# Norm sums inside the chunk loop, a reordered last unit and a two-tile start, in the dense layers of a two-block transformer kernel

## What is computed

```python
def rms_norm(x, gain):
    y = x * lax.rsqrt(jnp.mean(x * x, axis=-1, keepdims=True) + EPS)
    return y * gain

def conv_ffn(x, w_up, conv_w, conv_b, w_down):       # layers "ffn0" and "ffn1"
    hid = causal_dwconv(x @ w_up, conv_w, conv_b)
    gate, val = jnp.split(hid, 2, axis=-1)
    return (jax.nn.gelu(gate) * val) @ w_down

def swiglu(h, w_gate, w_up, w_down):                 # layer "ffn2"
    return (jax.nn.silu(h @ w_gate) * (h @ w_up)) @ w_down

# first block, twice:  mix -> x = x + rms_norm(mix, g[1]); h = rms_norm(x, g[2])
#                      x = x + rms_norm(conv_ffn(h), g[3])
# second block: mla attention + swiglu, then s5 mixer + mixture of 8 experts
```

## Time and profile before

| | us |
|---|---|
| median of 3 runs | 2239.53 |
| lowest, highest | 2238.09, 2240.12 |
| the profiled execution | 2240.73 |
| its span (first to last instruction) | 2238.6 |

### The profile page before, as it was taken

The page is one execution under the profiler, slowest core; times in us unless marked ns, Lnnn a source line. Parts: engine busy times, 40 slices in busy tenths (PEclk is TensorE's granted clock), DMA queues, the critical chain, the costliest instruction groups (busy, mean ns, idle before and its releaser), DMA issues.

```text
span 2238.6 us, 67369 instructions
## 1 busy us (share of the span) xinstructions
PE 2171.1 (97%) x30382; PEld 2005.3 (90%) x30382; DVE 847.0 (38%) x2103; ACT 467.1 (21%) x1074; POOL 24.5 (1%) x43
## 2 busy tenths in 40 slices
PE   9999999999999999999987999999999999999998
PEld 8888998757899876899976889999999999999998
DVE  4247665314867645567769220101010101010102
ACT  3432112113311135210033121111111111111112
POOL 1000000000000000000000000000000000000000
PEclk9899999999999999999998999999999999999999
DMA  9241444241244323343331259999999999999996
GB/s 391 90 169 64 163 170 159 74 181 58 113 164 154 136 79 132 151 156 153 150 127 59 93 182 405 392 396 392 397 389 399 393 395 391 397 383 396 388 417 262
DMA packets 78399, 535.02 MB, mean 239 GB/s; under 512 B 8913, under 2 KB 9042, under 8 KB 41938
## 3 DMA queue, kind: packets, MB, share of 16 engines
q1 hardware_dynamic: 74450, 519.82, 59.0%
q0 software_dynamic: 3840, 13.63, 1.7%
HBM read 523.20 MB, written 10.22 MB: 238 GB/s over the span
## 4 chain that ended last, share of the span: by engine, by line
PE 61%; DVE 3%; ACT 1%; issue 1%; DVEq 0%; ACTq 0%
PE ps L1792 26%; PE ps L1804 13%; PE ps L1179 6%; PE ps L1109 4%; PE ps L1212 4%; PE ps L1574 2%; PE ps L1557 1%; DVE scr L2467 0%; PE ps L1743 0%; PE ps L1756 0%; PE ps L1765 0%; PE ps L1444 0%; PE ps L1430 0%; PE ps L1511 0%; PE ps L1406 0%
## 5 line engine op out<-in xcount | busy, mean ns | idle before, releaser
L1792 PE MATMUL ps<-scr,slot 128*64 128x96 f32 x14336 | 638.1, 246 | 0.7 <-issue 0.7
L1792 PEld LDWEIGHTS ps<-scr,slot 128*64 128x64 f32 x14336 | 612.7, 137 | 2.4 <-issue 2.3
L2616 DVE TENSOR_TENSOR scr<-scr,ps 128x96 f32<-128x96 f32 x224 | 56.8, 254 | 764.9 <-ACT scr L960 764.9
L1804 PE MATMUL ps<-scr,slot 128*64 128x96 f32 x7168 | 341.9, 246 | 1.6 <-issue 1.6
L1804 PEld LDWEIGHTS ps<-scr,slot 128*64 128x64 f32 x7168 | 317.3, 137 | 1.8 <-issue 1.8
L1212 PE MATMUL ps<-scr,slot 128*128 128x256 f32 x1056 | 241.8, 383 | 7.9 <-DVE scr L2284 7.9
L1212 PEld LDWEIGHTS ps<-scr,slot 128*128 128x128 f32 x1056 | 198.0, 192 | 34.3 <-DVE scr L2284 9.5
L960 ACT ACTIVATE scr<-ps 128x96 f32<-128x96 f32 x224 | 56.1, 250 | 784.9 <-PE ps L1792 784.9
L1179 PE MATMUL ps<-vtok,slot 128*128 128x128 f32 x1056 | 140.1, 276 | 2.7 <-DVE vtok L2224 2.7
L1179 PEld LDWEIGHTS ps<-vtok,slot 128*128 128x128 f32 x1056 | 128.9, 192 | 3.5 <-DVE vtok L2224 3.5
L1179 PE MATMUL ps<-vtok,proj 128*128 128x128 f32 x1056 | 129.9, 277 | 0.0
(11 more groups left out here) (408 smaller groups left out, 2069.7 us busy)
## 6 DMA issues: line engine op xcount, KB each, us to landing
slot<-in_w_moe SPq DMA_DIRECT2D x224, 1024.0 KB, 7.0
slot<-in_w_moe SPq DMA_DIRECT2D x224, 512.0 KB, 7.0
slot<-in_w_ffn SPq DMA_DIRECT2D x33, 3072.0 KB, 10.4
slot<-in_w_even_in SPq DMA_DIRECT2D x3, 3072.0 KB, 27.2
slot<-in_w_odd_qk SPq DMA_DIRECT2D x2, 3072.0 KB, 10.8
slot<-in_w_s_glu SPq DMA_DIRECT2D x2, 3072.0 KB, 11.6
slot<-in_w_odd_v SPq DMA_DIRECT2D x2, 2048.0 KB, 8.0
slot<-in_w_even_in SPq DMA_DIRECT2D x2, 1536.0 KB, 10.7
```

The lines of the kernel that those rows point to most:

```text
L1792: m = pe.matmul(gate_up(j, k)[s:s + STRIP], ups[j][:, o:o + STRIP], xg[:, c], start=c == 0, stop=c == KD - 1, skip_group_check=True)
L1804: m = pe.matmul(y_sum(d)[s:s + STRIP], downs[j][:, o:o + STRIP], hid[j][:, 0:CAP], start=False, stop=False, skip_group_check=True)
L2616: dve.tensor_tensor(hid[f % 4][:, 0:CAP], gbuf[f % 4][:, 0:CAP], gate_up(f, 1), ALU.mult).then_inc(hid_ready, 1)
```

## The change

Three edits, in all places where they apply.

1. Input norm of the dense layers (n2, n6, m1). VectorE's adds of the squares go (`add_squares`, and in ffn2 the `add_square` calls), the three norms leave `PRESUMMED`, and TensorE sums all eight squares with the matrix of ones: the square of chunk c-1 behind the plain products of chunk c, that of chunk 7 at the end. `summed(0, 0)` then waits for each input sum by itself instead of for all four.
2. Last unit: up(10, 0), up(10, 1), down(9, 0), down(9, 1) instead of up, down, up, down.
3. `first_tiles`: the projections behind ffn0 and ffn1 fill tile 0 and tile 1 together, two products for each chunk of `hT`. In the fox projection tile 1 so comes before the eight gate products (L1455) and the norm's sum; before, it came after them.

```diff
-PRESUMMED = ("n1", "n2", "n3", "n4", "n5", "n6", "n7", "m0", "m1")
+PRESUMMED = ("n1", "n3", "n4", "n5", "n7", "m0")
...
+            def add_square(name, c):
+                if c == 0:
+                    pe.wait_ge(rms_ready, NORM_NO[name])
+                pe.wait_ge(sq_ready, SQ0[name] + c + 1)
+                m = pe.matmul(sum_of(name), ones[:, :], sq[:, c], start=c == 0, stop=c == KD - 1,
+                              skip_group_check=True)
+                if c == KD - 1:
+                    m.then_inc(sum_ready, 1)
...
+            def first_tiles(phase, name):
+                w, n = need(phase, 0), TILE0[phase]
+                pe.wait_ge(tile_taken, n + 2 - WORK)
+                for c in range(KD):
+                    pe.wait_ge(h_ready, H0[name] + c + 1)
+                    for i in range(2):
+                        o = (i * KD + c) * P
+                        m = pe.matmul(work(n + i), w[:, o:o + P], hT[:, c], start=c == 0,
+                                      stop=c == KD - 1, skip_group_check=True)
+                        if c == KD - 1:
+                            m.then_inc(tile_ready, 1)
...
+                    def inputs(n):
+                        if u == k == 0:
+                            pe.wait_ge(combined, X_SUM0[phase] + n)
                     pe.wait_ge(combined, W_SUM0[phase][2 * u + k] + 4)
+                    inputs(1)
                     four(k, P5, t1, s1, True)
+                    inputs(2)
                     four(k, P6, t2, s2, False)
...
                                   x_half[0][c // 4][:, c % 4], start=c == 0, stop=c % 4 == 3,
                                   skip_group_check=True)
-                presummed_total(LATE[phase])
-                pe.wait_ge(combined, X_SUM0[phase] + 4)
+                    if c:
+                        add_square(LATE[phase], c - 1)
+                add_square(LATE[phase], KD - 1)
                 summed(0, 0)
                 summed(0, 1)
                 for u in range(1, UNITS):
                     need(phase, u)
                     up(u, 0)
-                    down(u - 1, 0)
-                    up(u, 1)
+                    if u < UNITS - 1:
+                        down(u - 1, 0)
+                        up(u, 1)
+                    else:
+                        up(u, 1)
+                        down(u - 1, 0)
                     down(u - 1, 1)
...
             def fox():
-                linear("odd_qk", hT, h_ready, H0["n4"], range(1))
+                first_tiles("odd_qk", "n4")
...
                 presummed_total("n4")
-                linear("odd_qk", hT, h_ready, H0["n4"], range(1, 3))
+                linear("odd_qk", hT, h_ready, H0["n4"], range(2, 3))
...
             def mla():
-                linear("mla_in", hT, h_ready, H0["m0"], range(2))
+                first_tiles("mla_in", "m0")
...
-                    if c >= 3:
-                        add_square("m1", c - 2)
                 gain_tile("m1", KD - 1, "ffn_norm", 0)
-                add_square("m1", KD - 2)
...
             post_norm("n1", 8)
-            add_squares("n2")
             input_sums("ffn0")
...
             post_norm("n5", 40)
-            add_squares("n6")
             input_sums("ffn1")
```

More of the change, by code:

```diff
@@ L1191, in summed @@
                     s1, s2, s3, s4 = x_sum
+                    def inputs(n):
+                        if u == k == 0:
+                            pe.wait_ge(combined, X_SUM0[phase] + n)
                     pe.wait_ge(combined, W_SUM0[phase][2 * u + k] + 4)
+                    inputs(1)
                     four(k, P5, t1, s1, True)
+                    inputs(2)
                     four(k, P6, t2, s2, False)
+                    inputs(3)
                     four(k, P7, t3, s3, False)
+                    inputs(4)
                     four(k, P3, w_block(phase, u, k, 1, 1), s4, False)
```

## The result

The changed kernel takes 2226.4 us (median of four, 2223.3 to 2229.2) where the kernel before takes 2238.8 in the same session: a ratio of 0.9939 with an interval of 0.9924 to 0.9954. That is 13.7 us by the ratio and 12.4 by the medians, against 17.4 forecast. It is faster, and the time lies inside the stated range of 2217.5 to 2227.5, at its upper end. It lies outside the forecast's own range (2219.5 to 2224.5), and next to the 2226.7 of the rival by which the clock does not follow; that this rival's mechanism isn't what happened is shown further down.

A forecast was written before the change was run, and what follows sets the result against it. TensorE, busy for 97% of the span, bounds the kernel through its work, waits and low clock. -2.1 - 2.1 - 1.6 + 2.6 - 9.8 - 0.3 - 4.1 = -17.4 us from 2239.5 gives 2222.1, range 2217.5 to 2227.5.

The forecast's parts named there:

- the rival by which the clock does not follow: Stalls go, but the three low-clock stretches stay or turn up elsewhere; 4.7 us not gained, 2226.7 us; chance 0.17.
- Edit 1, squares between chunks: Start of ffn0 and ffn1: 0.875 us per chunk, input sums ready in time, new waits free; 2.1 us gained in each.
- The low clock in ffn1: Stretch behind ffn1's chunks, at a clock of 0.90: no gap, so no low clock expected after the change; 1.6 us gained.
- ffn2, +2.6: Start of ffn2: six more square products on the path, where VectorE's adds had been hidden; 2.6 us lost.
- Edit 2, -4.9 each and -0.3: Last unit: reordering removes a 3.3 us stall and 1.57 of low clock in ffn0 and ffn1; 0.3 gained in ffn2.
- The thin margin: Last unit of ffn0 and ffn1: two down products cover the chain to the hidden layer with only 0.1 us to spare.
- The rival by which the chain grows with the moved products: Last unit: the chain behind up(10, 1) grows, so only half of the 9.8 us is gained; 2227 us; chance 0.05.
- Edit 3, -2.15 and -2.05: Fox and mla projections: tiles 0 and 1 together take 6.9 us; 2.15 us gained in fox, 2.05 in mla.
- the mla margin: Mla projection: VectorE's adds end 0.3 us before the norm's sum is asked for; if used up, edit 3 gives 3.6.
- The clock term, 4.7 us: Low clock behind stalls goes: 1.6 us at ffn1's start plus 2 x 1.57 in the last units of ffn0 and ffn1.
- They shift as a block: Stages behind the layers (s5, router, experts) start from TensorE's events, weight loads too, so they move together; no loss there.
- The slower rival: Interleaved products run at 1.2 GHz, their 35 us of work taking 70; sum becomes +17, 2257 us; chance 0.02.

The follow-up runs named there:

- the version that undoes it: The changed kernel with ffn2's squares added on VectorE as before the change: 2222.8 us, ratio 0.9930 against the kernel before.
- the waits: The kernel before with 37 waits for something already there at the start of TensorE's program: 2242.0 us, ratio 1.0014.
- 104 instructions ahead: The changed kernel with ffn2's squares back on VectorE, plus 26 tiny unused products at the start of TensorE's program: 2223.5 us, ratio 0.9920.
- the single edits: Edits 1, 2 and 3 each made alone, against the kernel before: 2239.2, 2231.6 and 2236.3 us, ratios 0.9994, 0.9958 and 0.9990.

## Why the prediction was right where it was, and wrong where it wasn't

The terms inside the layers came true almost one by one. The number is too large by 4 to 5 us, because of the stages behind and, by an amount that stays open, the clock.

- **Edit 1, squares between chunks: right, with a gain forecast a little too large.** Chunks at the pace of 0.88 us, sums ready in time, waits at no cost. The piece took 7.33 us where 7.27 was worked out, and gained 1.9 in each layer where 2.1 was forecast. The rest is the cold weight load of 0.12 us, which I had counted with this piece and which lies behind its end (the -0.1 of unit 0 in the table).
- **The low clock in ffn1: 1.6 forecast, 1.7 in the first pair of profiles.** As a term of the time it holds only for some executions, see below.
- **ffn2, +2.6: right**, as 2.6 in three traces, and gone in the three of the version that undoes it. It was the one loss that was forecast, and it was real.
- **Edit 2, -4.9 each and -0.3: right** in all six traces that have it, against the first profile of before. Against the later profiles, whose stall brought no low clock, it is -3.4 each. The thin margin was as worked out. The rival by which the chain grows with the moved products falls: the hidden layer was there 0.2 us early.
- **Edit 3, -2.15 and -2.05: 2.0 each.** In fox the reciprocal came 1.5 us later from the projection's start, where 1.3 was worked out, and the margin of 1.2 was as forecast; the mla margin held.
- **The clock term, 4.7 us: too sure, by how much stays open.** I took three low stretches from one execution as if each execution had them. Over all profiles the odds are half for the last units and 5 in 14 for the chunk starts, each worth about 1.6: 1.6 x (2 x 6/12 + 2 x 5/14) = 2.7 us, so 2.0 less. In the sessions in which the changed kernel was timed the last units had it 6 times in 6 and the chunk starts 2 in 6, and the same sum gives 4.3, only 0.4 less. The rival "the clock does not follow" said that nothing of the 4.7 would be gained, since low stretches would stay or fall elsewhere. They didn't stay: none in 24 places behind the edits. Nor is there a sign that they fell elsewhere: outside the three layers, between 20 and 2200 us, the low clock cost 12 to 19 us (time multiplied by what the granted clock lacks to 1.00) in the six profiles with edit 1, and 12 to 22 in the seven without. That scatter, up to 10 us between executions, is why single profiles can't be compared by their spans.
- **"They shift as a block": the step that failed.** I looked for what the stages behind wait for and found TensorE's own events. They wait for TensorE's instructions, too, and where in the code that wait falls depends on how many instructions stand ahead, which edit 1 changes by 72: the wait moved from the projection tile into the burst of small products, where little work is left when the packet comes. The wait is 2.28 and 2.56 us where four profiles with nothing added ahead have 0.57, 0.38, 1.40 and 0.36. The start of s5 takes 15.3 and 17.3 us (the second with a low clock of 1.7 behind the wait), against 13.4 to 14.5, so 1.6 to 3.5 more than their mean. The sign is shown by time as well, since the kernel before became 2.2 us slower with 68 instructions ahead and 3.1 with the waits. No part of my sum or rivals had this term.
- **The rest.** -17.4 with 1.6 to 3.5 for s5 and 0.4 to 2.0 for the clock gives -11.9 to -15.4, against 12.4 to 13.7 measured. So the two terms are enough, but how they share the 4 to 5 us isn't shown. The experts' +4.6 in the first pair, of which 2.7 are in the last one, is no evidence for a loss by the change: the kernel before, unchanged, showed +6.0 and +2.7 there in its second profile, and the first profile's 112.4 us was the shortest of all. What follows is the last expert before, before again, and after:

```profile
2113.90:2226.30 112.40, 110.64 (x2639) 109.84 (x2639) 15.11 (x38) 16.34 (x36) 4.38 (x5) 1.00 0.91 368
```
```profile
2111.20:2226.30 115.10, 111.83 (x2639) 110.14 (x2639) 15.12 (x38) 16.38 (x36) 4.39 (x5) 1.00 0.91 360
```
```profile
2093.80:2208.90 115.10, 111.82 (x2641) 110.16 (x2639) 15.11 (x38) 16.40 (x36) 4.39 (x5) 1.00 0.91 360
```

- **The slower rival** asked for a low clock in the new loops; they have 1.00 throughout, as the window 160.30 to 167.60 above. The Trainium skill's rule on products that cycle through the banks (TensorE: Matmul & The Clock Gate, "A second HAM failure mode: psum-queue depth-cycling") did not show here, with three banks in turn. The page speaks of a TensorE that idles briefly between groups, and these loops had no idle time, so they don't test it.

**Left open:** what starts the 56th packet when it does, and so early with 104 instructions ahead; why 37 waits moved the place by 20 instructions; what decides whether a low clock follows idle time; how the missing 4 to 5 us are shared; and why edit 3's 4.0 us of trace gave 2.2 in time, if that is more than scatter.

## What to carry to other kernels

Fill a stall of the busiest engine by reordering before you think of making the chain shorter: one swap of two products, with a cover that exceeds the chain by 0.2 us, gave most of this change (9.4 of some 13 us). Moving an addition to the busiest engine pays only where that engine was standing still for it; the same edit gained 1.9 us twice where it stood still, and lost 2.6 where the additions had been hidden. And read a low clock, or a wait for instructions, from several executions, and from more than one session, before it enters a sum: one profile tells what can happen, the tally what it is worth.

## What the runs showed of the hardware

- **A wait for instructions has its place in the count of instructions.** Instructions come in packets of 16 KB on a queue of their own, one for 256. Around a burst of 64 small products (256 instructions in 1.3 us), TensorE waited 0.4 to 2.6 us, behind 7176 to 7178 matmuls in ten of thirteen profiles, whatever had been added or taken out: the place in the code moved by 46 instructions for 48 added, 56 for 56, 66 for 68, 68 and 70 for 72. With 256 added it was 128 matmuls later, so at the old place in the code. Two don't fit a plain count: 37 waits moved it by 20, and with 152 added (48 and 104) there was no wait. Each of the twelve waits ended 2.2 to 2.6 us after the start of one such packet. Edits far away can so make a stage slower or faster that nobody touched.
- **A low clock behind idle time comes in some executions only.** The same 3.15 us of idle time, in the same code, was followed by 7.17, 8.6 to 8.9 or 10.23 us for the same 32 matmuls: above 7.17 in 6 of 6 in the earlier sessions, and in 0 of 6 in the later ones, on another chip than the single edits. A wait for instructions can bring it as well (in s5 1.7 us more behind 2.56 and behind 2.07 us of waiting, none behind the other ten).
- **It also comes with no idle time in the records.** The 13.70 us in the fox attention had TensorE busy throughout, at a clock of 0.52; in the changed kernel 18 us ahead of the layers have 0.81:

```profile
92.00:110.00 18.00, 18.00 (x75) 14.50 (x75) 0.00 (x0) 3.46 (x7) 0.00 (x0) 0.81 0.33 141
```

- **Waits for things already there** cost nothing that shows among products (12 in the start of each layer), but 37 in a row ahead of the first product delayed it by 2.05 us, a delay that was gone by 12.4 us.
